# A Fourier, attention and top-2-of-8 expert encoder on one core: output projection by token blocks beside the router, token rows normalised on POOL, final weights ahead of the branch

## The reference, cut to what matters

```python
def rms_norm(x, g):
    return x * rsqrt(mean(x * x) + 1e-6) * g

# layer 0: Fourier mixing in 4 groups of 256 channels, then a dense SwiGLU of width 2816
u = rms_norm(h, norm_mix[0]) @ w_in                      # 1024 x 1024
h = h + real(fft2(u, over tokens and group channels, "ortho")) @ w_out
n = rms_norm(h, norm_ffn[0])
h = h + (silu(n @ w_gate) * (n @ w_up)) @ w_down
# layer 1: attention in 8x16 windows, 16 heads, then experts
qkv = rms_norm(h, norm_mix[1]) @ w_qkv
h = h + attention(qkv, rpb) @ w_o
t = rms_norm(h, norm_ffn[1])
logits = t @ router_w + router_b                         # 8 experts
top_val, top_idx = top_k(logits, 2); gates = softmax(top_val)
h = h + sum over the 2 chosen e of gates * (silu(t @ wg[e]) * (t @ wu[e])) @ wd[e]   # width 3584
out = rms_norm(h, final_norm)
```

## Time and profile before

| | us |
|---|---|
| median of 3 runs | 1365.94 (1365.29 to 1366.33) |
| the profiled execution, its own time | 1367.15 |
| its span, first to last instruction | 1365.3 |
| PE busy | 1344.7 (98%), 6341 instructions |
| DVE busy | 1111.9 (81%) |
| ACT busy | 923.2 (68%) |
| POOL busy | 34.5 (3%) |
| DMA | 432.32 MB, mean 317 GB/s |
| mean granted clock of PE | 0.992 |

### The profile page before, as it was taken

How to read it: one execution, slowest core, us unless ns; L and a number is a source line. 1 busy time by engine, 2 the same in 40 slices (tenths; PEclk the granted TensorE clock), 3 DMA queues, 4 the chain that set the end, 5 groups by cost and what they waited for, 6 DMA issues and landing times.

```text
span 1365.3 us, 17406 instructions
## 1 busy us (share of the span) xinstructions
PE 1344.7 (98%) x6341; PEld 1117.9 (82%) x6341; DVE 1111.9 (81%) x815; ACT 923.2 (68%) x755; POOL 34.5 (3%) x48
## 2 busy tenths in 40 slices
PE   8999999999999999999999999999999999999997
PEld 7888888787878888888888888888888888888885
DVE  5756666655678889888988988898898889889997
ACT  6554444545647778777777877877787787777774
POOL 0000000000101000000000000000000000002000
PEclk8999999999989999999999999999999999999999
DMA  9666775563339999999999999999999999999992
GB/s 354 246 207 179 210 211 190 175 204 104 101 109 378 383 378 365 395 382 357 398 388 372 373 394 377 358 398 388 368 376 394 367 370 397 381 374 385 396 394 90
DMA packets 194971, 432.32 MB, mean 317 GB/s; under 512 B 19632, under 2 KB 22064, under 8 KB 194800
## 3 DMA queue, kind: packets, MB, share of 16 engines
q1 hardware_dynamic: 178784, 416.28, 83.4%
q0 software_dynamic: 3360, 11.78, 2.2%
q10 hardware_dynamic: 12784, 3.69, 1.8%
HBM read 425.94 MB, written 5.78 MB: 316 GB/s over the span
## 4 chain that ended last, share of the span: by engine, by line
PE 95%; DVE 3%; ACT 1%; issue 1%; DMA 0%; POOL 0%; DVEq 0%; ACTq 0%
PE bank_G L1250 10%; PE bank_G L1252 10%; PE bank_G L1251 10%; PE bank_U L1250 10%; PE bank_U L1252 10%; PE bank_U L1251 10%; PE bank_Y L1250 8%; PE bank_Y L1252 8%; PE bank_Y L1251 8%; PE bank_T L1696 2%; PE bank_T L1250 1%; PE bank_T L1252 1%; PE bank_T L1251 1%; DVE w_lo L753 1%; PE bank_G L1512 0%
## 5 line engine op out<-in xcount | busy, mean ns | idle before, releaser
L753 DVE TENSOR_TENSOR w_lo<-raw,w_hi 128x2048 fp32r<-128x2048 f32 x390 | 885.9, 2289 | 184.6 <-ACT w_hi L458 183.8
L458 ACT ACTIVATE w_hi<-raw 128x2048 fp32r<-128x2048 f32 x390 | 748.6, 1920 | 276.6 <-PE bank_U L1252 98.2
L1250 PE MATMUL bank_Y<-w_hi,hidT_hi 128*128 128x512 f32 x492 | 192.2, 391 | 0.0
L1252 PE MATMUL bank_Y<-w_hi,hidT_lo 128*128 128x512 f32 x492 | 191.6, 389 | 0.0
L1251 PE MATMUL bank_Y<-w_lo,hidT_hi 128*128 128x512 f32 x492 | 191.5, 389 | 0.0
L1250 PE MATMUL bank_U<-w_hi,xg_hi 128*128 128x512 f32 x448 | 179.1, 400 | 0.0
L1250 PE MATMUL bank_G<-w_hi,xg_hi 128*128 128x512 f32 x448 | 175.2, 391 | 1.3 <-DVE xg_lo L774 0.9
L1252 PE MATMUL bank_U<-w_hi,xg_lo 128*128 128x512 f32 x448 | 175.0, 391 | 0.0
L1251 PE MATMUL bank_U<-w_lo,xg_hi 128*128 128x512 f32 x448 | 174.5, 390 | 0.0
L1252 PE MATMUL bank_G<-w_hi,xg_lo 128*128 128x512 f32 x448 | 174.5, 390 | 0.0
L1251 PE MATMUL bank_G<-w_lo,xg_hi 128*128 128x512 f32 x448 | 174.4, 389 | 0.0
(11 more groups left out here) (301 smaller groups left out, 1363.5 us busy)
## 6 DMA issues: line engine op xcount, KB each, us to landing
raw<-in_expert_w_gate SPq DMA_DIRECT2D x112, 1024.0 KB, 7.7
raw<-in_expert_w_up SPq DMA_DIRECT2D x112, 1024.0 KB, 7.8
raw<-in_expert_w_down SPq DMA_DIRECT2D x112, 1024.0 KB, 7.7
raw<-in_nat_w_qkv SPq DMA_DIRECT2D x12, 1024.0 KB, 5.1
raw<-in_ffn_w_gate SPq DMA_DIRECT2D x11, 1024.0 KB, 8.9
raw<-in_ffn_w_up SPq DMA_DIRECT2D x11, 1024.0 KB, 5.7
raw<-in_ffn_w_down SPq DMA_DIRECT2D x11, 1024.0 KB, 5.2
raw<-in_fourier_w_out SPq DMA_DIRECT2D x4, 1024.0 KB, 15.6
```

Source lines behind the costliest of these rows:

```text
L458: nc.scalar.activation(w_hi[w][:], raw[s][:], ACT.Copy).then_inc(hi_made, 1)
L753: nc.vector.tensor_tensor(w_lo[w][:], raw[s][:], w_hi[w][:].bitcast(f32), ALU.subtract).then_inc(lo_made, 1)
L1250: nc.tensor.matmul(out_, xh, wh, start=start, stop=False)
L1252: return nc.tensor.matmul(out_, xl, wh, start=False, stop=stop)
```

## The change

- Start: `still(23)` for `still(12)`.
- Fourier: `token_dft` goes round four banks (T0, T1, G0, G1) and waits for `pt_lo` of m-4; `channel_dft` has a bank per group (Y0, Y1, U0, U1).
- Stream 1 and 2: the first products wait for one quarter of `act_lo` at a time.
- Output projection: h is summed per block and column half; `transpose_tokens_of(b, half)` takes the place of `transpose_stream(3, half)`, and the last product is cut in two around one of them. The norm's gains are multiplied into the router's weights (`rw_scaled`, DVE) and no longer into the activations. Logits go per block. DVE's split of piece W0+5 moves from ahead of the router to behind the first gather. `keep_warm(12)` and `keep_warm(5)` for 6 and 2.
- The token rows are normalised on POOL by four operations of 128x1024 (times `rstd`, times the gains, per block), no longer by two on DVE.
- Expert 7: `gates` (3 operations) stays at step c = 1, the other 3 of `gate_weights` go to the last gate step. The last piece is split by column halves; the last `down` is done by column halves, with the scatter of the first half between products of the second.
- Final norm: squares by column half on ACT, h times the final weights on DVE ahead of the branch, times `rstd` on ACT, output from other buffers.

```diff
-        rstds(3)
+        for b in range(NB):
+            pool.wait_ge(sq_done, NB * 3 + b + 1)
+            ...   # rstd of block b, as before
+        pool.wait_ge(s_gain, 32)
+        for b in range(NB):
+            pool.wait_ge(rstd_done, 3 + b + 1)
+            pool.wait_ge(h_half, 4 + 2 * b + 2)
+            nc.gpsimd.tensor_scalar(hn[:, b], h[:, b], rstd[:, 3, b:b + 1], None, ALU.mult).then_inc(hn_scaled, 1)
+            pool.wait_ge(hn_scaled, b + 1)
+            nc.gpsimd.tensor_tensor(hn[:, b], hn[:, b], mo["gain"][:, 0], ALU.mult).then_inc(hn_made, 1)
...
-        still(12)
+        still(23)
...
-            if m >= 2:
-                pe.wait_ge(pt_lo_done, m - 1)
+            if m >= 4:
+                pe.wait_ge(pt_lo_done, m - 3)
...
+                        if stream is not None and b == 0 and kk % 2 == 0:
+                            pe.wait_ge(act_lo_done, 4 * stream + kk // 2 + 1)
...
-        wo_product(0, 1, 0)
-        wo_product(0, 1, 1)
-        wo_product(1, 1, 0)
-        transpose_stream(3, 0)
-        wo_product(1, 1, 1)
+        wo_product(0, 1, 0)
+        wo_product(1, 1, 0)
+        transpose_tokens_of(0, 0)
+        wo_product(0, 1, 1)
+        transpose_tokens_of(0, 1)
+        last_wo_product()          # transpose_tokens_of(1, 0) in its middle
         pe.wait_ge(rw_lo_done, 1)
-        pe.wait_ge(act_lo_done, 4 * 3 + 2)
-        ...
-        keep_warm(6)
+        logits(0, 0)
+        transpose_tokens_of(1, 1)
+        logits(0, 1)
+        logits(1, 0)
+        logits(1, 1)
+        keep_warm(12)
...
-        keep_warm(2)
+        keep_warm(5)
...
+        # DVE, from the output projection on
+        split_past(W0 + 1)
+        add_wo(0, 0)
+        split_past(W0 + 2)
+        add_wo(0, 1)
+        squares_of_rest(0)
+        tokens_lo(0, 0)
+        token_lo(0, 0)
+        add_wo(1, 0)
+        tokens_lo(0, 1)
+        token_lo(0, 1)
+        tokens_lo(1, 0)
+        add_wo(1, 1)
+        squares_of_rest(1)
+        tokens_lo(1, 1)
...
         select(0, 0)
+        token_lo(1, 0)
         token_lo(1, 1)
...
-        for b in range(NB):
-            nc.vector.scalar_tensor_tensor(out=hn[:, b], in0=h[:, b], scalar=rstd[:, 3, b:b + 1], in1=mo["gain"][:, 0], ...)
...
+            if kept:
+                last_columns(0, 4)         # last down: all 12 products of Y0
+                last_columns(1, 2)         # 6 products of Y1
+                scatter(0)
+                last_columns(1, 2, 2)      # 6 products of Y1
...
+        # ACT, behind the branch
+        for b in range(NB):
+            act.wait_ge(fin_rstd, b + 1)
+            for q in range(2):
+                act.wait_ge(fin_gain, 2 * q + b + 1)
+                part = FINAL[b][:, BANK * q:BANK * (q + 1)]
+                nc.scalar.activation(part, part, ACT.Copy, scale=rstd[:, 4, b:b + 1]).then_inc(fin_scaled, 1)
```

More of the change, by code:

```diff
@@ L1160, in expert @@
                     hidden_rest(E, c - 1)
+                if (kind, c, half) == ("gate", STEPS - 1, 1) and kept and not sweep:
+                    gate_weights()
                 if (kind, c, half) == ("gate", 1, 1) and ahead and not sweep:
@@ L1203, in _ @@
         assert made[0] == N1
-        for b in range(NB):
-            nc.vector.scalar_tensor_tensor(out=hn[:, b], in0=h[:, b], scalar=rstd[:, 3, b:b + 1], in1=mo["gain"][:, 0],
-                                           op0=ALU.mult, op1=ALU.mult).then_inc(hn_made, 1)
         for j in range(SPLIT, AHEAD):
@@ L1252, in three, with project @@
             return nc.tensor.matmul(out_, xl, wh, start=False, stop=stop)
-        def project(pieces, banks, width, done, before=lambda n, b: None):
+        def project(pieces, banks, width, done, before=lambda n, b: None, stream=None):
             for n, j in enumerate(pieces):
@@ L1720, in down, with last_columns, scatter @@
                 last.then_inc(piece_used, 1)
+            def last_columns(q, rows, first=0):
+                c = STEPS - 1
+                if first == 0:
+                    ready(AT["down", c, 0], E)
+                    pe.wait_ge(e_hidT_lo, E * STEPS + (c + 1))
+                for kk in range(first, first + rows):
+                    half, k = kk // KROW, kk % KROW
+                    j = AT["down", c, half]
+                    if q == 0 and half and k == 0:
+                        pe.wait_ge(lo_half, E - LAST + 1)
+                    if q == 1 and half and k == 0:
+                        ready(j, E)
+                    wh, wl = parts(j, E, KROW)
+                    cs = slice(BANK * q, BANK * (q + 1))
+                    last = three(Y[q][:], hidT_hi[c % 2][:, P * kk:P * (kk + 1)], hidT_lo[c % 2][:, P * kk:P * (kk + 1)],
+                                 wh[:, k, cs], wl[:, k, cs], False, kk == BANK // P - 1)
+                    if q and k == KROW - 1:
+                        last.then_inc(piece_used, 1)
+                    elif kk == BANK // P - 1:
+                        last.then_inc(e_y, 1)
+            def scatter(q):
+                pe.wait_ge(e_selT_copy, E - LAST + 1)
+                pe.wait_ge(e_ylo, 2 * (E - LAST) + 1 + q)
+                for b in range(NB):
+                    cs = slice(BANK * q, BANK * (q + 1))
+                    bk = T[q] if b == 0 else (G, U)[q][1]
+                    nc.tensor.matmul(bk[:], mo["selT"][:, b], mo["y_hi"][:, cs], start=True, stop=False)
+                    nc.tensor.matmul(bk[:], mo["selT"][:, b], mo["y_lo"][:, cs], start=False, stop=True).then_inc(e_scatter, 1)
             for c in range(STEPS):
```

285 lines of the change are left out of this document (162 added, 123 removed).

## The result

| | before | after |
|---|---|---|
| median | 1366.05 us (1364.59 to 1367.38, 20 runs) | 1368.59 us (1366.86 to 1369.56, 20 runs) |
| ratio, 95% interval | | 1.0018, 1.0011 to 1.0024 |
| profiled execution, its span | 1367.15, 1365.3 | 1368.72, 1366.9 |

The account below looks back on a forecast made before the run. PE was taken as the bound, busy 98% of the span. Gains of 2.1, 0.8, 3.2, 0.55 and 0.2 sum to 6.85 us, taken from the 1365.94 median: 1359.1 us, range 1357.5 to 1364.5.

Parts of the forecast that it names:

- Start and Fourier: Kernel start and Fourier stage: more zero products keep the clock up and four banks remove a wait; gain 2.1 us.
- the second wait for `pt_lo`: Fourier stage, ahead of the last `channel_dft`: PE's 0.7 us idle there was to remain.
- Quarter waits: Ahead of qkv's first products: starting on the first quarter of `act_lo` cuts PE's 1.36 us idle; gain 0.8 us.
- Router without POOL: Output projection to first gate: the two-largest chain begins 3.3 us earlier; the stage gains 3.2 us net.
- Token rows on POOL: Beside the router: POOL's four row operations take 5.6 us, scaled from a memset, and cost nothing.
- At zero it is costed: POOL's token rows: cost zero, since the gather for expert 1 needs them only a whole expert later, 100 us free.
- rivals 1 and 3: Router: POOL's row operations hold DVE's two-largest chain; 1363.4 us at chance 0.27, or with slower POOL 1370.4 at 0.08.
- Rival 3: Router: slow POOL operations hold DVE; a loss from 9.6 us for the four, 1370.4 us at 14; chance 0.08.
- The clock's 1.0: Router: PE's clock falls around 388 to 391, so warming products at half clock outlast the chain; about 1.0 us lost.
- Expert 7: Expert 7's start: three gate-weight operations moved away remove PE's wait for `w_lo`; gain 0.55 us.
- The end: Last product to output: later second half outweighed by smaller squares, earlier scaling and ACT's scalings; net gain 0.2 us.
- The 1.2 of the start's clock: Kernel start: the part of the 2.1 us gain credited to the clock, 1.2 us, the banks giving 0.9.

Follow-up runs that it names:

- rows_on_dve: The changed kernel with the token rows normalised by DVE again, POOL's four row operations gone: 1363.59 us, 0.9984 to before.
- pool_one_input: The changed kernel with POOL's two-input row operations made one-input tensor_scalars times 1.0, leaving out the norm's weights: 1362.49 us, 0.9978 to before.
- rows_in_gaps: The changed kernel with the end as before, token rows on DVE in four halves in its idle gaps, 9 warming passes for 12: 1359.87 us, 0.9958.
- end_final_dve: The changed kernel without the early products with the final weights and ACT's scaling; DVE does both at the very end: 1368.86 us, 1.0018 to before.
- best_scatter_behind: rows_in_gaps with squares by halves, first scatter still behind the last down product, final scaling on DVE: 1361.24 us, 0.9961 to before.

## Why the prediction was wrong

- **Start and Fourier: right, against the one execution.** 2.1 forecast, 1.99 measured; `channel_dft(0)` forecast at 35.05, found at 35.06 with no half-clock product, and the second wait for `pt_lo` stayed. The gap behind the zero products became 0.5 (8.2 to 8.66), not 0.9, and the granted clock stayed at 1.00 through it. One reading was wrong and did no harm: the clock's column in the earlier trace rows is at 1.00 both at 3.5 and at 4.5, so it doesn't show the rise that I had put near 4.5.
- **Quarter waits: right.** 0.8 forecast, 0.79 measured, 0.58 of wait left.
- **Router without POOL: right.** 3.3 earlier was forecast for the chain; 388.16 with the 2.8 us of the stages ahead is 390.98, forecast 390.8. rows_on_dve gains 3.4 in the stage, 3.2 forecast. W0+5 costs 0.28, forecast 0.2.
- **Token rows on POOL: the step that failed.** "At zero it is costed" held for the data and fell for the engine beside it. Two things were wrong. The size: I scaled a memset to 5.6 us for four operations, and they took 10.4. An operation that only writes was no ruler for one that reads, and 0.94 became 2.86. The Trainium skill's figure for two inputs ("GPSIMD Engine Reference", section 3.1) agrees with the trace: half of 4497 ns for half the length, 2.37 found; the one-input operation, which section 4.1 calls roughly line-rate, was the slower of the two. The chance: rivals 1 and 3 were the same mechanism, with 0.35 between them, because one `pow` behind a scaling on DVE seemed to speak against it. That was one operation of one element. The same rows showed POOL held by DVE, and a hold seen in one direction should have been priced in both.
- **The rivals' time came out, in part by luck.** Rival 3 put the point of loss at 9.6 us for the four and 1 us of time on each further us: 10.4 makes 1366.7. With the 2.1 us by which the end was missed that is 1368.9, measured 1368.6. "Over 1368 would mean POOL's operations above 2.4 us each": they are 2.6 in the mean, but by the same working that alone makes only 1366.7, and it took the end's 2.1 to come over 1368. Its picture was too simple: the chain doesn't crawl behind POOL to its end, but stops at each two-input operation and runs almost free in between (`used` at 393.4, POOL's end at 396.3), the last of these holds falls on `slot`, and `sel` is held by the memset, which no rival had.
- **The clock's 1.0: right without POOL.** In rows_on_dve it fell where it was expected (granted 0.50 from 388 to 390), and the warming products outlast `used` by 1.1. In after they end before the held `used`, so this term cost nothing; but its gather ran at half clock, behind 1.7 and 1.6 us in which PE idled in the hold. In rows_on_dve, pool_one_input and rows_in_gaps PE doesn't idle there, and the gather is at full clock.
- **Expert 7: right.** 0.55 forecast, 0.41 measured.
- **The end: wrong by 2.1.** 0.2 gained was forecast, 1.92 lost. The second half came 1.35 later, counted from the last `hidT_lo`, and 1.3 was forecast; end_final_dve against best_scatter_behind gives 1.1 for this order. What I had set beside it was wrong: of the square's 0.43 and the 0.6 of DVE's late start, 0.8 went into POOL's tensor_scalar, held under products that I had counted as free; ACT's four scalings took 2.56 in place of 2.74, not 0.5 less; and the last output landed 2.9 after its issue in place of 2.2, for which the sum had no term and no run shows a cause. The hold that I knew from the earlier trace rows was not applied to an operation that the change adds.
- **The base.** The sum was made against an execution 1.1 above the median and subtracted from the median. The 1.2 of the start's clock are in that execution and in part of the others only, so the median could not fall by as much. This would have cost a right forecast some 1 us.

## What to carry to other kernels

Moving work to POOL "for nothing" was nearly free here only where POOL's operation reads one operand, or where DVE beside it reads PSUM or reduces, and even POOL's memset of 0.97 us held two small DVE steps for 0.6; a two-input operation on POOL stops a chain of small SBUF-to-SBUF steps on DVE for its whole length, and a 0.2 us step becomes 2 us. Look for the gaps that the chain itself leaves on DVE: here four halves of 0.75 us fitted into them and beat both kernels. An order that gives an early half a head start pays for it with the late half, where the end hangs on the late one.

## What the hardware showed that I had not expected

- POOL's 128x1024 tensor_scalar with one input from SBUF took 2.83 to 2.86 us, its tensor_tensor with two took 2.35 to 2.37.
- During POOL's tensor_tensor, DVE's tensor_tensor and tensor_scalar on SBUF waited for its end (2.08, 2.27, 1.42, 1.47 us for steps of 0.17), while tensor_reduce (0.17) and operations with an input from PSUM (`logit`, 0.48 for two) ran on. The Trainium skill, "SBUF — State Buffer", section "Who interferes with whom", says this of two-input operations and excepts tensor_reduce and, outside its two-port modes, those with at most one input in SBUF. The trace agrees for the two-input operations and for tensor_reduce; `slot` is a tensor_scalar with one input and was held all the same, which that section allows only in a two-port mode, and no run shows the mode.
- During POOL's memset of 1x1024 (0.97), which writes and reads nothing, the two `sel`, tensor_scalars of 128x128, took 1.10 for 0.48.
- During POOL's tensor_scalar the same steps waited only until about 1.1 us from its start (0.95, 1.06, 0.43) and then took 0.17 each for the 1.7 us left. The same section of the Trainium skill says, of DVE's two-port modes, that the first to issue has the shared pair for the whole instruction; for this pair of engines and operations the measurement differs.
- The reverse hold is real: POOL's tensor_scalar of one element took 0.98 us for 0.19 under two products on DVE, and one of 128x1024 took 4.97 for 2.86 under splits.
